# The remaining projections of two transformer blocks as three fp32r products, with GpSimd making the low parts of the weights

## What is computed

```python
proj = h @ w_in[l]
y_pool = y_pool @ w_pool_up[l]
y_attn = y_attn @ w_attn_up[l]
merged = jax.nn.sigmoid(m_pool) * y_pool + jax.nn.sigmoid(m_attn) * y_attn
x = x + gate[:, None, :] * (merged @ w_out[l])
```

## Time and profile before

| | |
|---|---|
| median of 3 executions | 1305.66 us (1304.69 to 1307.52) |
| the profiled execution, its time | 1305.09 us |
| its span in the trace | 1303.2 us |
| TensorE matmuls busy | 1236.8 us |
| VectorE, ScalarE, GpSimd busy | 855.0, 564.0, 420.7 us |
| granted TensorE clock, mean | 0.974 |

### The profile page before, as it was taken

How to read it: one execution, slowest core, us unless ns; L and a number is a source line. 1 busy time by engine, 2 the same in 40 slices (tenths; PEclk the granted TensorE clock), 3 DMA queues, 4 the chain that set the end, 5 groups by cost and what they waited for, 6 DMA issues and landing times.

```text
span 1303.2 us, 18456 instructions
## 1 busy us (share of the span) xinstructions
PE 1236.8 (95%) x6978; PEld 1015.2 (78%) x6978; DVE 855.0 (66%) x1818; ACT 564.0 (43%) x1027; POOL 420.7 (32%) x231
## 2 busy tenths in 40 slices
PE   5899999888989989999999999999999999999996
PEld 2778864344555469999999999999888888888885
DVE  5678734444345542699958988999756666656666
ACT  2454411112232333544455666655455554545553
POOL 0968700000000000588877777776500000000000
PEclk9899999898979989999999999999999999999998
DMA  9987844433231323365554545554466666666654
GB/s 377 417 321 297 322 185 164 152 133 158 99 128 65 143 116 130 105 188 179 184 188 147 163 162 157 155 159 148 146 233 192 225 225 217 198 191 193 195 192 150
DMA packets 54519, 244.23 MB, mean 187 GB/s; under 512 B 6944, under 2 KB 7328, under 8 KB 42016
## 3 DMA queue, kind: packets, MB, share of 16 engines
q1 hardware_dynamic: 54000, 242.34, 53.9%
q10 hardware_dynamic: 432, 0.72, 0.2%
HBM read 240.94 MB, written 2.10 MB: 186 GB/s over the span
## 4 chain that ended last, share of the span: by engine, by line
PE 91%; DVE 4%; ACT 1%; issue 1%; DMA 1%; SPq 0%; POOL 0%; POOLq 0%; DVEq 0%
PE bank L1376 9%; PE bank L1373 9%; PE bank L1372 9%; PE bank L1001 6%; PE banks L1001 6%; PE banks L1412 4%; PE bank L1412 4%; PE banks L1418 4%; PE bank L1418 4%; PE banks L1415 4%; PE bank L1415 4%; PE banks L1386 3%; PE bank L1049 2%; PE bank L1053 2%; PE bank L1057 2%
## 5 line engine op out<-in xcount | busy, mean ns | idle before, releaser
L711 POOL TENSOR_TENSOR split_r<-ring,split_r 128x1024 fp32r<-128x1024 f32 x128 | 307.6, 2404 | 159.8 <-ACT split_r L921 159.7
L921 ACT ACTIVATE split_r<-ring 128x1024 fp32r<-128x1024 f32 x256 | 269.2, 1052 | 180.4 <-PE bank L1376 180.4
L1372 PE MATMUL bank<-h_high_r,split_r 128*128 128x256 f32 x1024 | 251.2, 283 | 1.7 <-ACT split_r L921 1.7
L1373 PE MATMUL bank<-h_low_r,split_r 128*128 128x256 f32 x1024 | 251.1, 283 | 0.0
L1952 DVE TENSOR_TENSOR split_r<-ring,split_r 128x1024 fp32r<-128x1024 f32 x128 | 156.8, 1225 | 65.6 <-ACT split_r L921 65.6
L1372 PEld LDWEIGHTS bank<-h_high_r,split_r 128*128 128x128 f32 x1024 | 195.8, 191 | 1.9 <-issue 1.9
L1373 PEld LDWEIGHTS bank<-h_low_r,split_r 128*128 128x128 f32 x1024 | 195.9, 191 | 0.0
L1376 PE MATMUL bank<-h_high_r,split_r 128*128 128x256 f32 x1024 | 143.7, 283 | 0.2 <-POOL split_r L711 0.2
L1376 PEld LDWEIGHTS bank<-h_high_r,split_r 128*128 128x128 f32 x1024 | 132.0, 192 | 0.4 <-POOL split_r L711 0.4
L975 ACT ACTIVATE gs_r<-G 128x256 fp32r<-128x256 f32 x128 | 53.5, 418 | 172.6 <-PE bank L1418 172.6
L715 POOL TENSOR_TENSOR small<-small 128x1 f32<-128x1 f32 x2 | 1.5, 759 | 359.0 <-DVE small L1978 359.0
(11 more groups left out here) (382 smaller groups left out, 2042.8 us busy)
## 6 DMA issues: line engine op xcount, KB each, us to landing
ring<-in_down SPq DMA_DIRECT2D x128, 512.0 KB, 3.5
ring<-in_up SPq DMA_DIRECT2D x128, 512.0 KB, 3.5
G<-in_ada SPq DMA_DIRECT2D x32, 1024.0 KB, 10.5
G<-in_in SPq DMA_DIRECT2D x32, 1024.0 KB, 7.1
G<-in_out SPq DMA_DIRECT2D x8, 1024.0 KB, 8.4
G<-in_wq SPq DMA_DIRECT2D x8, 1024.0 KB, 6.0
tab<-in_ada SPq DMA_DIRECT2D x4, 1024.0 KB, 5.6
G<-in_poolup SPq DMA_DIRECT2D x2, 1024.0 KB, 6.3
```

The lines of the kernel that those rows point to most:

```text
L711: pool.tensor_tensor(wsplit[:, j % SPLIT, 1, :], raw[:, j % RAW, :], wsplit[:, j % SPLIT, 0, :].bitcast(F32), ALU.subtract).then_inc(low_r ...
L921: nc.scalar.activation(wsplit[:, n % SPLIT, 0, :], raw[:, n % RAW, :], ACT.Copy).then_inc(high_ready, 1)
L1372: mm(o, w[0][:, c, :], h_high[:, c, :], start=(c == 0), stop=False)
L1373: mm(o, w[0][:, c, :], h_low[:, c, :], start=False, stop=False)
```

## The change

13 more panels become 26 units, numbers 20 to 45: both up projections, both output projections and all of `in2`. What `project` did for them is now done by three new ways:

- `products`, as before for `in1`, for the up projections and for `in2` 0 to 3 (new step `unit`): 24 calls for a unit, both token tiles together. For an up projection the order is now column half by column half, each for both token tiles; before it was token tile by token tile.
- `row_high` and `row_low` for both output projections, `in2` 5, `in2b` and `in2` 4 (`BY_ROWS`): one token tile at a time, 24 calls over both units, the product with the low activations last.
- The first tile of `in2` 5 does its `row_high` ahead of the other tile's transposes (`proj_head`).

Steps `("high", k)` are put into the order for ScalarE's copies of 2048 columns. GpSimd makes the low part of each unit in four instructions, in the order of its own list: units to 29, then the two powers of the turn-over, 30 to 33, the eight `kv_twice` copies, 34 to 43, the power of `gn`, 44 and 45. The activations are split where they leave their PSUM bank: ScalarE copies the high part, VectorE subtracts it from the bank (`upT`, `oT`, `mT`), or from `hT` (`xlow`). Nothing of this exists for `hT` of block three, which is as it was.

Besides: the scaling of x (two instructions of 1024 columns) moves from `normed` to a step `xout` behind `xlow`; ScalarE's squares of `xg` go to a PSUM bank; three DMAs that ScalarE issues move from the turn-over to behind `in2` 4; in block two's heads `head_norm` i-1 comes ahead of `head_mask` i; the sums of `ada2` 5 all stand in the heads; four of the `kvT` steps move together; `in2` 0 to 3 fill banks 4 and 5; the iterations' lists are written anew, so that `gate` 0 and `mT` 1,0,0 now stand in one iteration.

Cut to its core:

```diff
+SPLIT_PANELS += [("poolup", None), ("attnup", None), ("out1", 0), ("out1", 1), ("in2", 5), ("in2b", None), ("in2", 4)]
+SPLIT_PANELS += [("in2", i) for i in range(4)] + [("out2", 0), ("out2", 1)]
+BY_ROWS = [("out1", 0), ("out1", 1), ("in2", 5), ("in2b", None), ("in2", 4), ("out2", 0), ("out2", 1)]
...
+        out.extend([("wout", b, 0, 0), ("wout", b, 0, 1)])
+        if b == 0:
+            out.append(("high", 29))
+        out.extend([("wout", b, 1, 0), ("var", b, 0), ("norm", b, 0), ("wout", b, 1, 1),
...
+              [("upT", 0), ("upT", 1), ("high", 22), ("up", "poolup", 0, 0), ("up", "poolup", 1, 0)]]
...
+    out.append(("high", 23))
+    out.extend(("up", "poolup", t, 1) for t in range(NT))
...
+    out.extend([("high", 24), ("high", 25)])
+    out.extend(("up", "attnup", t, half) for half in range(2) for t in range(NT))
...
+    turn_over(0, [("xlow", 0), ("proj_head", "in2", 5, 0)])
+    out.extend([("xlow", 1), ("xout",)])
+    out.extend(("high", k) for k in range(30, 34))
+    out.extend(("proj", "in2", 5, t) for t in range(NT))
...
+    out.extend([("high", 34), ("high", 35), ("kvT", 2), ("kvT", 0), ("kvT", 1), ("unit", 34), ("nqT", 0), ("nqT", 1), ("kvT", 3),
+                ("high", 36)])
...
+        [("unit", 35), ("half", "in2", 0, 0), ("half", "in2", 0, 1), ("blk", 0), ("blk", 1), ("high", 37)],
         [("hid", 0)],
-        [("half", "in2", 1, 0)],
...
+        [("ret", 0), ("ret", 1), ("cmpT", 0), ("cmpT", 1), ("sum", n, 6)],
+        [("retO", 0), ("retO", 1), ("ret", 2), ("ret", 3), ("cmpO", 0), ("cmpO", 1), ("sum", n, 7)],
+        [("retO", 2), ("retO", 3), ("gn",), ("high", 44)],
+        [("gate", 0), ("mT", 1, 0, 0), ("high", 45)],
         [("wout_head", 0)],
...
+            for u in range(30):
+                unit_low(u)
...
+            for u in range(30, 34):
+                unit_low(u)
...
+            for u in range(34, 44):
+                unit_low(u)
...
+            for u in range(44, 46):
+                unit_low(u)
...
+            def x1_high_part(t, half):
+
+                evacuated(act, ("xT", 1, t, half))
+                c, tok = slice(4 * half, 4 * half + 4), slice(t * P, (t + 1) * P)
+                nc.scalar.activation(x1_high[:, c, tok], hT[1][:, c, tok], ACT.Copy).then_inc(x1_high_ready, 1)
...
-                    dst = mT[b][:, 4 * half:4 * half + 4, t * P:(t + 1) * P]
-                    bank_free(nc.scalar.activation(dst, src[:, :].rearrange("p (c n) -> p c n", c=4), ACT.Copy), s)
+                    dst = mT_high[b][:, 4 * half:4 * half + 4, t * P:(t + 1) * P]
+                    nc.scalar.activation(dst, src[:, :].rearrange("p (c n) -> p c n", c=4), ACT.Copy).then_inc(m_high_ready, 1)
...
-                        ins = nc.scalar.activation(xg_squares[:, t, c], xg[:, t, c], ACT.Square, accum_out=sqg[:, t, half:half + 1])
+                        ins = nc.scalar.activation(ps[4 + 2 * half + t][:, :], xg[:, t, c], ACT.Square, accum_out=sqg[:, t, half:half + 1])
...
-                if s == ("norm", 0, 1):
+                if s == ("proj", "in2", 4, 1):
...
+            def row_high(units, o, tok, x_high, x_ready):
+
+                for k in units:
+                    half = UNITS[k][1]
+                    _, w_high, w_low = unit_views(k)
+                    pe_.wait_ge(split_high, k + 1)
+                    x_ready(half, 0)
+                    for c in range(4):
+                        mm(o, x_high[:, 4 * half + c, tok], w_high[:, c, :], start=(half == 0 and c == 0), stop=False,
+                           skip_group_check=True)
+                    wait_low(pe_, k)
+                    for c in range(4):
+                        mm(o, x_high[:, 4 * half + c, tok], w_low[:, c, :], start=False, stop=False, skip_group_check=True)
+
+            def row_low(units, o, tok, x_low, x_ready):
+
+                for k in units:
+                    half = UNITS[k][1]
+                    _, w_high, _ = unit_views(k)
+                    x_ready(half, 1)
+                    for c in range(4):
+                        ins = mm(o, x_low[:, 4 * half + c, tok], w_high[:, c, :], start=False, stop=(half == 1 and c == 3),
+                                 skip_group_check=True)
+                return ins
+
...
+                    if s[1:3] == (1, 0):
+                        units, o = units[1:], ps[USE[s][0]][:, :]
+                    else:
+                        o = bank_to_fill(pe_, s)[:, :]
+                    row_high(units, o, tok, mT_high[b], m_ready(b, t))
+                    bank_full(row_low(units, o, tok, mT_low[b], m_ready(b, t)), s)
...
-                    ts(xv[:, t, :], xg[:, t, :], r_pair[:, t, 0:1], None, ALU.mult).then_inc(x_ready, 1)
...
+                    if s[1] > 8:
+                        head_norm(s[1] - 1)
                     head_mask(s[1])
-                    if s[1] not in (0, 8):
...
+                elif kind == "xlow":
+                    t = s[1]
+                    tok = slice(t * P, (t + 1) * P)
+                    dve.wait_ge(x1_high_ready, 2 * t + 2)
+                    for half in range(2):
+                        evacuated(dve, ("xT", 1, t, half))
+                    tt(x1_low[:, :, tok], hT[1][:, :, tok], x1_high[:, :, tok].bitcast(F32), ALU.subtract).then_inc(x1_low_ready, 1)
+                elif kind == "xout":
+                    for t in range(NT):
+                        ts(xv[:, t, :], xg[:, t, :], r_pair[:, t, 0:1], None, ALU.mult).then_inc(x_ready, 1)
...
+                elif kind == "mT":
+                    _, b, t, half = s
+                    src = bank_read(dve, s)
+                    c, tok = slice(4 * half, 4 * half + 4), slice(t * P, (t + 1) * P)
+                    turned_high(dve, s)
+                    bank_free(tt(mT_low[b][:, c, tok], src[:, :].rearrange("p (c n) -> p c n", c=4),
+                                 mT_high[b][:, c, tok].bitcast(F32), ALU.subtract), s)
                 elif kind == "o":
...
```

228 lines of the change are left out of this document (135 added, 93 removed).

## The result

| | before | after |
|---|---|---|
| median (range) | 1306.04 us (1304.69 to 1307.52), 6 executions | 1297.87 us (1294.73 to 1300.41), 6 executions |
| ratio, 95% interval | | 0.9937 (0.9921 to 0.9953) |
| the profiled execution: time, span | 1305.09, 1303.2 us | 1300.41, 1298.6 us |

The change makes the kernel 8.2 us faster. I had forecast 1284.0, 22 us faster. 1297.87 lies at the very end of the range. (The table ahead of the prediction has the first three of the six executions before, hence its 1305.66.) The executions of the changed kernel scatter over 5.7 us, those of the kernel before over 2.8, and the profiled one is the slowest of its six.

A forecast was written before the change was run, and what follows sets the result against it. TensorE's work plus its waits and low-clock time was taken as the bound. Terms -35.5 + 7.5 - 2.3 + 10 - 1 - 2.4 + 2 = -21.7 took 1305.1 to 1283.4, median 1284.0 us; range 1271 to 1298.

The forecast's parts named there:

- The price of a call: Converted TensorE calls: three fp32r products take 0.681 us instead of 0.859 for one plain fp32 call; 35.5 us less work.
- A, +7.5: Up projections and first output projection: later copies, a wait for VectorE's merging and low clock cost 7.5 us.
- B, -2.3: Turn-over and `in2` 5: old waits go, late power, late copy and clock remain; 8.4 us against 10.7.
- C, +10: `in2b` and `in2` 4: bank wait 4 us, low part 33 late by 3.6, clock 2.4; between 3 and 13.
- D and E, -1.4: From `in2` 4 to the first `hid`, -1 us; the heads, -2.4 and +2.
- I leave 7 of the 17.9 for waits and clock: Heads: of 17.9 us waits and clock before, 7 stay, since norm ahead of mask lets pT go at once.
- +2 for ten units' 40 GpSimd instructions: Heads: GpSimd's low-part instructions stop a head's chain here and there, 2 us, range 0 to 13.
- the hole: Behind score 23 in the heads: TensorE idles 8.5 us (6 to 11) while `mT` 1,0,0 waits for `gate` 0 on VectorE.
- `hid` 0: Right behind `in2` 0: TensorE waits 5.3 us (3 to 9) for rope, gate and `blk` from VectorE.
- F, 0: Last output projection and the turn-over behind it: no cost beyond the calls already counted; the wait for the turn-over stays.
- rival 2: Heads become a VectorE chain: GpSimd instructions hit masks and norms TensorE waits for, +11 us, 1295; chance 16%.
- Rival 1: Waits stay small because VectorE and GpSimd seldom meet; about 12 us less, 1272; chance 20%.

The follow-up runs named there:

- cut-in-two run: Changed kernel with each GpSimd low-part instruction from unit 20 on cut in two (256 or 140 columns): 1301.43 us, ratio 0.9973 to the kernel before.
- thin low parts: Changed kernel, GpSimd low parts on 16 columns, low-weight correction left out: units 20 to 45 but 41, 1279.83 us; units 20 to 33 alone, 1289.62 us.
- plain fp32: Changed kernel with units 34 to 41 (`in2` 0 to 3) as plain fp32 products again, without copies or low parts: 1299.84 us, ratio 0.9942 to the kernel before.
- the power moved: Changed kernel with the first token tile's power ahead of low part 29 on GpSimd instead of behind it: 1296.89 us, ratio 0.9928 to the kernel before.
- the second profile: Profile from running the changed kernel once more, with nothing changed: median 1298.11 us, ratio 0.9925 to the kernel before.

## Why the prediction was wrong

- **The price of a call: right.** 0.681 for 0.859 us, 35.5 us in all; the split shows 35.0. Groups of 8 calls stand 1.81 us apart in after, as in the earlier trace rows.
- **A, +7.5: right in sum (+8.2).** The wait before `mT` was 2.6 instead of 3.9, the clock's share larger (3.1 for 2.3).
- **B, -2.3: -1.0.** Power and copy were named in the right places, 4.3 and 2.2 us for 1.4 and 3.4. I had not seen that three low parts in a row would be stretched by VectorE (17.70 us for twelve instructions instead of 15.1).
- **C, +10: +6.6.** The bank wait was 3.9 for 4, the clock 2.7 for 2.4. Low part 33 was not late (3.6 forecast); the cut-in-two run shows how near it was (6.1 us).
- **D and E, -1.4: +15.0. This is the step that failed**, in two terms. First, "I leave 7 of the 17.9 for waits and clock". Nothing supported that cut: the waits of block two's heads that are not the hole came to 5.7 us in E alone, and the clock's loss in E to 18.1. I took the change's new order of norm and mask for a cure of waits that have other causes (the two longest of them, 3.5 us, are for ScalarE's copies of `rT` behind a head's exponentials). Second, "+2 for ten units' 40 GpSimd instructions": thin low parts in the heads give 9.5 us back, waits and clock together, so this overlaps with the first term. The mechanism was in my text and in the earlier trace rows; I priced it as stops of a head's chain here and there, when 28.5 us of VectorE's time went to it over the stretch. The hole (10.2 for 8.5) and `hid` 0 (6.0 for 5.3) were well sized, and what the clock lost behind them was small (1.7 and 2.7). The clock was lost behind waits of 1 to 2 us and once behind none, 13.6 us in all, and for these my sum had no term but the 7.
- **F, 0: right.**

That the result is still inside the range is partly luck: the error in C, 3.4 us the other way, hides some of that in the heads. What came out is nearest to rival 2, "the heads become a VectorE chain", 1295 at 16%. It named the place and a cause that the runs with thin low parts and with plain fp32 bear out; the clock it did not name. Rival 1 relied on the first 180 us, where the same scheme has few gaps; why it has few was not tried.

## What to carry to other kernels

When work is taken off the busiest engine, price each wait that stays as wait plus low clock (behind a wait of 1.0 us the clock lost 3.4 us, behind one of 10.2 us only 1.7), and ask of every stage that has waits whether the work was only their cover: here a third of the conversion brought nothing measurable. Before giving an idle engine work, count the other engine's instructions that it will stop, in both directions; moving one step out of the overlap (the copy of unit 37) took 2.3 us from a wait, with a median 4 us lower at the edge of the noise; cutting the instructions in two cost 3.6. Work that nobody reads, put where TensorE waits, keeps its clock and gave about 5 us in both kernels, but only where it needs no bank that is itself waited for.

## What was not expected of the hardware

- The clock falls behind some waits of 1.0 to 1.3 us and not behind others of the same length at the same place: in the changed kernel's profile it was low from 408 to 416 us behind a wait of 1.02 us, in that with the power moved it stayed high there behind 1.02 us, which makes 3 us of difference in the stretch. From 391 to 398 us it was low behind no wait at all, 3.4 us lost, and 5.1 in the second profile.
- Between VectorE and GpSimd both lose: VectorE 28.5 us over the stretch, GpSimd 2.6 us in twelve instructions beside the output projection, and 2.6 us in eight half-size ones beside a column sum (8.22 for 5.62).
- The code ahead of the stretch took between 177.95 and 187.89 us in profiles in which TensorE and VectorE have the same work up to there. The latest, that of the thin low parts, shows one cause. Far ahead of the edit a VectorE subtraction that takes 1.42 us at this place in the changed kernel stood for 7.55 us, while GpSimd made six low-part pieces at its full pace (1.24 us each); the copy that frees TensorE's bank is behind it, and TensorE idled 6.2 us instead of 1.1:

```profile
57.49 9.93 POOL L720 TENSOR_TENSOR wq_low_r<-G,G_r 128x512 fp32r<-128x512 f32 x8
59.94 7.55 DVE L1610 TENSOR_TENSOR G<-G,ring 128x64 f32<-128x64 f32 x1
67.55 0.54 DVE L1769 COPY G<-bank 128x384 f32<-128x384 f32 x1
```

  So VectorE does not always get its turn behind one GpSimd instruction. This is the only VectorE instruction over 3 us before 500 us in any of the profiles. Whether the executions of this kernel near 1289 us (others are at 1274 to 1282) all have such a stop, no run shows.
